# Second mixer of a two-layer decoder step: the norm's weights multiplied into twenty weight panels by ScalarE, in pieces, in place of GpSimd

## What is computed

```python
kv = rmsnorm(h, norm_kv) @ w_kv                       # keys and values, 16 heads of 64
q = (rmsnorm(h, norm_mix[1]) @ w_q_b[0])              # queries
z = q k^T * 64**-0.5 + bias
log1mb = where(mask, log_sigmoid(-z), 0)
a = exp(where(mask, z + cumsum(log1mb, reverse), -inf))
h = h + (a @ v) @ w_out_b[0]
```

## Time and profile before

| | |
|---|---|
| median of 3 runs | 2898.7 us |
| profiled execution | 2903.9 us, span 2901.8 us |
| second mixer, whole pairs | from 1347.7 us, 92.7 us a pair |
| TensorE busy in such a pair | 90.7 of 93.0 us |
| VectorE, ScalarE, GpSimd busy | 59.9, 54.4, 16.5 of 93.0 us |
| GpSimd's multiplications (L158) | 24, 1.9 us each |

### The profile page before, as it was taken

The page is one execution under the profiler, slowest core; times in us unless marked ns, Lnnn a source line. Parts: engine busy times, 40 slices in busy tenths (PEclk is TensorE's granted clock), DMA queues, the critical chain, the costliest instruction groups (busy, mean ns, idle before and its releaser), DMA issues. The chain is left out here.

```text
span 2901.8 us, 49032 instructions
## 1 busy us (share of the span) xinstructions
PE 2824.4 (97%) x19713; PEld 2601.3 (90%) x19713; DVE 1297.3 (45%) x1854; ACT 824.2 (28%) x1679; POOL 732.1 (25%) x449
## 2 busy tenths in 40 slices
PE   7999999999999999999999999998899999999998
PEld 7988889999999999997777777775899999999998
DVE  6423345433333333356656766566543333333333
ACT  5221123201110011125555665556320111001112
POOL 3212112232232232242112121111222332332331
PEclk9999999999999999999999999998999999999999
DMA  5675545223223223234444344434311111111112
GB/s 171 190 162 181 102 32 111 88 88 102 87 87 101 87 87 101 87 118 117 118 116 128 107 136 114 132 96 117 119 48 48 44 45 49 43 45 49 43 47 78
DMA packets 361447, 277.23 MB, mean 96 GB/s; under 512 B 31378, under 2 KB 352914, under 8 KB 359250
## 3 DMA queue, kind: packets, MB, share of 16 engines
q1 hardware_dynamic: 340074, 261.97, 31.6%
q10 hardware_dynamic: 21224, 13.15, 2.6%
HBM read 251.06 MB, written 91.11 MB: 118 GB/s over the span
## 5 line engine op out<-in xcount | busy, mean ns | idle before, releaser
L162 POOL CAST w_hi<-w_raw 128x1024 fp32r<-128x1024 f32 x193 | 206.2, 1068 | 1549.3 <-PE bank L216 877.2
L214 PE MATMUL bank<-x_hi,w_hi 128*128 128x352 f32 x1536 | 495.6, 323 | 1.7 <-PEq L2406 1.7
L214 PE MATMUL bank<-p_u_hi,w_hi 128*128 128x352 f32 x1536 | 495.4, 323 | 0.0
L215 PE MATMUL bank<-p_u_lo,w_hi 128*128 128x352 f32 x1536 | 492.7, 321 | 0.0
L215 PE MATMUL bank<-x_lo,w_hi 128*128 128x352 f32 x1536 | 492.4, 321 | 0.0
L216 PE MATMUL bank<-p_u_hi,w_lo 128*128 128x352 f32 x1536 | 492.2, 320 | 0.0
L216 PE MATMUL bank<-x_hi,w_lo 128*128 128x352 f32 x1536 | 492.1, 320 | 0.0
L166 POOL TENSOR_TENSOR w_lo<-w_raw,w_hi 128x1024 fp32r<-128x1024 f32 x193 | 467.9, 2424 | 28.9 <-DVE p_u_lo L2310 14.7
L2254 ACT ACTIVATE p_u_hi<-p_relu 128x352 fp32r<-128x352 f32 x192 | 95.6, 498 | 1192.4 <-DVE p_relu L2307 1192.4
L2316 DVE TENSOR_TENSOR h<-bank,h 128x352 f32<-128x352 f32 x384 | 201.3, 524 | 489.2 <-PE bank L216 489.2
L214 PEld LDWEIGHTS bank<-x_hi,w_hi 128*128 128x128 f32 x1536 | 288.1, 188 | 2.8 <-issue 2.8
(11 more groups left out here) (286 smaller groups left out, 4438.9 us busy)
## 6 DMA issues: line engine op xcount, KB each, us to landing
k_pages<-in_cache_k SPq DMA_DIRECT2D x64, 512.0 KB, 5.8
w_raw<-in_w_up SPq DMA_DIRECT2D x64, 512.0 KB, 4.1
v_pages<-in_cache_v SPq DMA_DIRECT2D x64, 512.0 KB, 4.8
w_raw<-in_w_down SPq DMA_DIRECT2D x64, 512.0 KB, 3.4
p_pages<-k_pages SPq DMA_DIRECT2D x256, 128.0 KB, 2.4
p_pages<-v_pages SPq DMA_DIRECT2D x256, 128.0 KB, 2.4
w_raw<-in_w_in_a SPq DMA_DIRECT2D x25, 512.0 KB, 4.0
h_spill<-h SPq DMA_DIRECT2D x16, 528.0 KB, 7.0
```

The costliest lines, as they stand in the source:

```text
L162: pool.tensor_copy(m.whi[slot][:, :], m.wraw[slot][:, :]).then_inc(w.hi, 1)
L214: pe.matmul(bank[:, 0:TW], wh, xh, start=(k == 0), stop=False)
L215: pe.matmul(bank[:, 0:TW], wh, xl, start=False, stop=False)
```

## The change

From panel 4 on, GpSimd no longer multiplies. ScalarE does it in place in `w_raw`, as 8 activations of 128 x 128 with a column of the norm's weights as scale (`norm_rows`), two behind each turn's reading and its gates: panel 3p+4 in slot -1 of pair p (slot 7 of the pair before), 3p+5 in slot 4, 3p+6 in slot 5. The first piece waits for the load, the last one increments `panel_normed`, on which GpSimd's split now waits in place of the load. Two loads are issued earlier: 3p+4 in slot -2 (slot 6 of the pair before) and 3p+5 in slot 0.

```diff
-    WEIGHTS_AT, STORES_AT = {0: 4, 1: 5, 4: 6}, {2: "values", 6: "keys"}
+    WEIGHTS_AT, STORES_AT = {-2: 4, 0: 5, 4: 6}, {2: "values", 6: "keys"}
+    NORMED_AT, NORMED_FROM = {-1: 4, 4: 5, 5: 6}, 4
...
             for n in range(2, len(panels)):
-                pool.wait_ge(w.loaded[n % 2], (n // 2 + 1) * 16)
+                if n < NORMED_FROM:
+                    pool.wait_ge(w.loaded[n % 2], (n // 2 + 1) * 16)
+                else:
+                    pool.wait_ge(normed, n - NORMED_FROM + 1)
 
                 pool.wait_ge(w.tile_ready, (n - 1) * NT)
                 if n % 3 == 1:
 
                     pool.wait_ge(a_ready, unit_no(n // 3 - 1, 2, 0, 0))
-                split_panel(pool, m, w, n, n % 2, panels[n][2])
+                split_panel(pool, m, w, n, n % 2, panels[n][2] if n < NORMED_FROM else None)
...
+            def norm_rows(no, kk):
+
+                if kk == 0:
+                    act.wait_ge(w.loaded[no % 2], (no // 2 + 1) * 16)
+                rows = m.wraw[no % 2][:, kk * P:(kk + 1) * P]
+                last = act.activation(rows, rows, ACT.Copy, scale=panels[no][2][:, kk:kk + 1])
+                if kk == KT - 1:
+                    last.then_inc(normed, 1)
...
                 turns = turns_of(slot)
+                panel_rows = [(3 * q + x, kk) for q, x in at(NORMED_AT, slot) if 3 * q + x < len(panels) for kk in range(KT)]
...
                     read_turn(y)
                     if due and (due[0][0] == 0 or i):
                         gates(p, n, *due.pop(0))
+                    for x in panel_rows[2 * i:2 * i + 2]:
+                        norm_rows(*x)
...
                 for x, h2 in due:
                     gates(p, n, x, h2)
+                for x in panel_rows[2 * len(turns):]:
+                    norm_rows(*x)
```

More of the change, by code:

```diff
@@ L1496, in mixer_b @@
         y_hi, y_x = own.sem("y_hi_ready"), own.sem("y_split")
-        filled, chain = own.sem("fills"), own.sem("dve_step")
+        filled, chain, normed = own.sem("fills"), own.sem("dve_step"), own.sem("panel_normed")
         turned, turn_read = own.sem("turned"), own.sem("turn_read")
```

## The result

The changed kernel takes 2902.2 us (median of 22 runs, 2899.05 to 2905.7); the kernel before takes 2896.8 us beside it (22 runs, 2894.39 to 2900.2). The ratio is 1.0018, 95% interval 1.0011 to 1.0024. That is some 5 us more, less than the 5.8 us that the text called no change, and inside the range of 2895 to 2907. But it is four times the forecast of 1.3 us, and the interval lies above 1. So there is something to find.

What follows compares the result with a forecast made beforehand. TensorE was taken to bound the kernel, busy 90.7 of 93 us a pair. Removal 0, relief 0, pieces +1.3 in slot -1 and moved loads 0 gave +1.3 on 2898.7: 2900.0 us, range 2895 to 2907.

Steps and rivals of the forecast that it cites:

- Removal from GpSimd: 20 multiplications of 1.90 us leave GpSimd in the mixer; panels are not late, so an earlier split is worth 0.
- VectorE's relief: VectorE regains up to 5.7 us a pair, but TensorE does not wait for it: 0, far end 16 us.
- Rival 2: VectorE paces the mixer's pairs after all: faster, half of TensorE's waits gone gives 2892.0 us; chance 0.05.
- Pieces in slots 4, 5 and 7: ScalarE's added pieces, 0.28 us each, fit its idle time in these slots of a pair: cost 0.
- Rival 3: ScalarE backs up in slot 4, past TensorE's next turn: 3.5 us slower over 7 pairs, 2903.5 us; chance 0.04.
- Slot -1: Ahead of the first pair, without fill, pieces between four page reads delay the first scores by 1.3 us.
- Moved loads: Key panel's load ahead of slot 7's pages: first page lands after 4.6 us, barely in time, 0; far end 12.6 us.
- Rival 1: Slot 7's first page late behind the panel: one us late is +6, all 2.1 give 2912.6 us; chance 0.10.
- The sum: Terms 0 - 0 + 1.3 + 0 = +1.3 us on the profiled span, set on the median of 2898.7: 2900.0 us.
- the boundary: Start of the phase behind the mixer, where TensorE waits for the third output panel's split; taken as unchanged, no term.
- The last pair: The mixer's last pair, where TensorE has no fill, gets neither pieces nor panels; taken as unchanged, 0.

Runs made afterwards that it cites:

- f4: Changed kernel with panels 4 to 23 multiplied by nobody, and ScalarE's third to eighth `h` reload held until the third output panel landed; 2902.67 us, ratio 1.0020.
- e3: Kernel before with only the loads of key and value panels moved, GpSimd multiplying as before; 2898.20 us, ratio 0.9999.
- g1: Kernel before with the third and fourth output panels loaded by SyncE at the end of the mixer; 2896.01 us, ratio 0.9988.
- h1: Kernel before with eight idle 128 x 128 ScalarE activations in slot -1, to delay all that follows; 2898.87 us, ratio 1.0000.
- e1: Kernel before once more, unchanged, for a second trace; 2896.19 us, ratio 0.9996.
- f1: Kernel before with ScalarE's third to eighth reload of `h` held until the third output panel landed; 2902.40 us, ratio 1.0016.
- g2: Changed kernel with the third and fourth output panels loaded by SyncE at the end of the mixer; 2896.49 us, ratio 0.9993.
- e2: Changed kernel once more, unaltered; 2901.39 us, ratio 1.0009 to the kernel before.
- f2: Changed kernel with ScalarE's third to eighth reload of `h` held until the third output panel landed; 2903.10 us, ratio 1.0022 to the kernel before.
- f3: Changed kernel with panel 4's pieces at the end of slot -2, and ScalarE's third to eighth `h` reload held until the third output panel landed; 2902.78 us, ratio 1.0020.
- e4: Changed kernel with panel 4 left to GpSimd, so no pieces in slot -1; 2897.93 us, ratio 1.0005 to the kernel before.

## Why the prediction was right, and where it was short

**Removal from GpSimd, 0: right.** The pair and its waits are what they were, in the changed kernel and in f4.

**VectorE's relief, 0: right.** Its 7.5 us a pair exceed the 5.7 that the text allowed, since more than the products was stretched: the scans lost 5.1 us. None of it reached TensorE. Rival 2 wanted pairs of 91.5 us or less; they are 92.7 at the least.

**Pieces in slots 4, 5 and 7, 0: right.** The room at TensorE's next turn in slot 4 is 0.53 us, the text had 0.59 left (1564.54 - 1563.95). Rival 3 falls. A piece lasts 0.39 to 0.47 us in the trace, the text had 0.37 to 0.39; but what counts is the distance from read to read, and that came out at 1.06 for 1.04. Two pieces and the overlap with the read make 0.59 us, 0.295 a piece. The Trainium skill, "ScalarE: Activation LUTs", section "What ACT_TABLE_LOAD costs", gave an estimate of 0.29; on this the page was nearer than my 0.28 from the earlier trace rows, by 0.03 us a pair of pieces.

**Slot -1, +1.3: right.** 1.35 in the profiled execution, and the wait of 1.47 us in every trace with the pieces there; where panel 4's pieces are elsewhere it is 0.67 or 0.68. From GpSimd's clearing to the first key split the four traces of the changed mixer have 56.1 to 56.3 us, and those with no work of ScalarE added in slot -1 54.7 to 54.9.

**Moved loads, 0: right to a few tenths.** A page behind one panel takes up to 4.9 us in the changed kernel and 5.4 in e3, not 4.6, so the room was used up now and then: 0.5 us in e3, and for values' pages 0.2 in the changed kernel. Two of its six periods are 93.04 and 92.84 us instead of 92.7, 0.4 us in all. I can't put these down to the moved loads, though: g1, whose mixer has the old loads, has a period of 93.05, and h1 one of 93.34, with a wait of 0.4 us for a page of keys that has no panel in front of it. The six periods together are 556.4 us in the three other traces with the old loads (before, e1, f1), 556.7 in g1 and 557.0 in h1, and 556.5 to 557.3 in the nine with the moved ones. Rival 1 exists, but what was seen of it is 0.5 us of the 12.6 at its far end.

**The sum, +1.3 of some 5: short.** The step that failed is the last one of the working: the terms were added up and everything behind the mixer was taken to follow unchanged. It had no term for the boundary, though a wait of 5.3 us stood there in the trace of before, for a panel that landed after 13.1 us instead of 4 to 6. In the mixer (g2 over g1) there are 0.5 to 0.8 us; at the boundary (g1 and g2 against the kernels without the early load) there are 4.8 of 5.3 us by the medians and 2.9 of 3.7 by the means. That the sum's 1.3 comes near the mixer's part is in part luck, as the last pair shows below.

**What stays open.** Why the changed mixer makes the boundary longer is not shown. The delay by itself does not (h1), the moved loads by themselves do not (e3, though its interval reaches to 1.001), and the boundary of e2's one traced execution is short, with 3.0 us, while the kernel's times are long. One difference runs through the traces: SyncE's load of the panel is issued 0.2 us behind ScalarE's first reload of `h` in the changed kernel, e2, f2 and f3, and 0.5 us behind it in the kernel before, e1, e3, e4, f1, f4 and h1. That is a correlation with the kernel and not with the wait, which is 3.0 and 5.4 us at the shorter distance and 3.0 to 7.3 at the longer one; and I made no run that sets this distance. As only first executions are traced, the boundary of the runs that make up the medians was not seen.

**The last pair, 0: not as forecast.** It has neither pieces nor panels to fill with, and the text took it to be unchanged. It was not, and the profiled spans differ by only 0.5 us for this reason. From 1907 to 2056 us, the last pair and the end of the mixer, the mean clock was 0.94 of full speed before and 0.97 after, and the lag of 2.2 us at the last key panel's split (1906.32 against 1904.08) had shrunk to 0.3 at SyncE's load of the output panel (2057.02 against 2056.74). The changed mixer has 0.97 there in all four of its traces (the changed kernel, e2, f2, g2); all the other kernels have 0.94 or 0.95, but for e3 with 0.97. From the last key split to ScalarE's first reload of `h` the changed mixer has 150.4 to 150.6 us in these four, the kernel before and g1 152.1 and 152.4, e1 and f1 151.3. So in the traces the whole mixer, from GpSimd's clearing to that reload, is 763.3 to 763.7 us in the changed kernels and 762.5 to 763.9 with the mixer of before: what slot -1 costs is mostly won back here. Why the clock is higher there is not shown (e3 has it by the moved loads alone, 150.2 us, but e4 and f4, which move them too, have 151.4 and 152.6). In the comparison of g1 and g2 this gain is contained.

## What to carry to other kernels

Work that moves off an engine nobody waits for gives nothing, and it costs where it lands in a place without fill: here six small instructions between four reads, worked out to 0.05 us from rows of the trace. Behind the last stage that a change touches, look at the next wait that is already there: where it hangs on a load that is issued together with bulk traffic, it can differ by more than the change itself, and it scatters the runs. Here a mixer that costs 1 us more went with 5 us in the medians, by a way that is not shown. Look at means and tails beside medians too. Taking such a wait out (g1) is both the better experiment and the better kernel: g1 has the lowest median of all that ran here and is 0.1% below the kernel before by the ratio, and the change brings nothing on top of it.

## What the runs showed of the hardware that I had not expected

- A load of 512 KB that is issued beside eight of 528 KB on another engine's queue lands after 13.1 us, where the same size lands after 4.1 to 6.3 in the mixer; a load of 128 KB behind one of 512 KB lands after up to 4.9 (5.4 in e3) instead of 2.3.
- The wait that follows from it is 3.0 to 7.3 us in executions of kernels whose code there is the same, and the clock of the stretch behind it goes with it: 0.95 or 1.00 of full speed from 2065 to 2100 us after 3.0 us of waiting, 0.85 after 7.3.
- With that wait gone, the kernel before scatters over 4 us (12 runs), and over 6 to 16 with it (samples of 12 to 35 runs). Most of the scatter of this program went with one load.
- Two scans of 256 columns that run wholly beside GpSimd's rounding and subtraction take 4.18 us, although the multiplication ahead of them is gone. ScalarE's pieces have no such partner that the traces show: VectorE is busy for 51.8 us from 1438.12 to 1530.85 us in the changed kernel, and for 54.4 in f4, which has no pieces but whose value and query panels are split at other times in the pair. The Trainium skill, "SBUF — State Buffer", section "Who interferes with whom", has it so: ScalarE waits on nobody, and VectorE's instructions with two inputs in SBUF share a read port with GpSimd. The 7.5 us a pair by which VectorE's busy time fell agree with the second part.
